# Convolution bias and gating bias taken off TensorE: added by VectorE, with the shifted weights made on ScalarE and GpSimd

## The reference

```python
def conformer_conv(a, gate, conv_w, conv_b, ln_g, ln_b):
    u = a * jax.nn.sigmoid(gate)
    u = lax.conv_general_dilated(            # depthwise, 31 taps, 512 channels
        u, conv_w[:, None, :], window_strides=(1,), padding=[(15, 15)],
        dimension_numbers=('NWC', 'WIO', 'NWC'), feature_group_count=D_A) + conv_b
    return jax.nn.silu(layernorm(u, ln_g, ln_b))

def spatial_gating(u, v, v_ln_g, v_ln_b, spatial_w, spatial_b):
    # out = u * (W_s norm(v) + b) within chunks of 128 positions, 4 heads of 128
    vn = layernorm(v.reshape(bn, s, N_SGU, H_D), v_ln_g, v_ln_b)
    vn = vn.reshape(bn, s // CHUNK, CHUNK, N_SGU, H_D)
    sv = jnp.einsum('hqk,bnkhc->bnqhc', spatial_w, vn) + spatial_b.T[:, :, None]
    return u * sv.reshape(bn, s, D_D)
```

## Time and profile before

| | us |
|---|---|
| median of 3 runs | 2552.85 |
| profiled execution, its own time | 2555.56 |
| its span, first to last instruction, slowest core | 2553.8 |
| spans of the 8 cores | 2547.6 to 2553.8 |

### The profile page before, as it was taken

How to read it: one execution, slowest core, us unless ns; L and a number is a source line. 1 busy time by engine, 2 the same in 40 slices (tenths; PEclk the granted TensorE clock), 3 DMA queues, 4 the chain that set the end, 5 groups by cost and what they waited for, 6 DMA issues and landing times.

```text
span 2553.8 us, 38161 instructions; the slowest of 8 cores (2547.6 to 2553.8 us)
## 1 busy us (share of the span) xinstructions
PE 2516.9 (99%) x12591; PEld 1184.0 (46%) x12591; DVE 894.7 (35%) x1454; ACT 619.6 (24%) x1083; POOL 413.6 (16%) x708
## 2 busy tenths in 40 slices
PE   8999999999999999999999999999999999999998
PEld 5445444444444444444444474444444444444443
DVE  4487465222222222211234773232223222222112
ACT  4336341131211121111143453211111111111111
POOL 3212233011101110010124521110111011101100
PEclk9999999999999999999999999999999999999999
DMA  8976799766645994456362278983576457644522
GB/s 176 192 128 146 148 150 177 159 148 123 127 141 120 159 158 141 104 75 103 125 117 95 43 143 172 168 148 114 120 128 112 120 120 127 113 120 98 76 42 99
DMA packets 310221, 323.98 MB, mean 127 GB/s; under 512 B 146049, under 2 KB 268177, under 8 KB 309906
## 3 DMA queue, kind: packets, MB, share of 16 engines
q0 software_dynamic: 123488, 121.41, 34.0%
q1 hardware_dynamic: 181506, 195.40, 28.0%
q10 hardware_dynamic: 5040, 4.73, 0.6%
HBM read 325.96 MB, written 79.69 MB: 159 GB/s over the span
## 4 chain that ended last, share of the span: by engine, by line
PE 95%; DVE 2%; DMA 1%; issue 1%; ACT 1%; POOL 0%; DVEq 0%; ACTq 0%; POOLq 0%
PE ps L171 95%; DMA wd<-ffn_wd 1%; DMA w_in<-ev_w_in 0%; DVE bst L1005 0%; DVE psum_w L755 0%; ACT BIG L1025 0%; ACT vn L1025 0%; DVE hb L379 0%; DVE gT L496 0%; DVE vt L1359 0%; ACT tmp L494 0%; DVE mv L1008 0%; DVEq L33 0%; DVE bst L1344 0%; DVE A L410 0%
## 5 line engine op out<-in xcount | busy, mean ns | idle before, releaser
L171 PE MATMUL ps<-BIG,wgu 128*128 128x512 bf16 x5632 | 1226.2, 379 | 0.0
L171 PEld LDWEIGHTS ps<-BIG,wgu 128*128 128x128 bf16 x5632 | 550.6, 98 | 662.7 <-issue 1.1
L171 PE MATMUL ps<-wd,gT 128*128 128x512 bf16 x2816 | 610.9, 380 | 2.1 <-DMA wd<-ffn_wd 2.1
L496 DVE TENSOR_TENSOR gT<-tmp,ps 128x512 bf16<-128x512 f32 x352 | 242.0, 687 | 812.7 <-PE ps L171 780.4
L171 PEld LDWEIGHTS ps<-wd,gT 128*128 128x128 bf16 x2816 | 276.0, 98 | 335.7 <-issue 4.5
L494 ACT ACTIVATE tmp<-ps 128x512 f32<-128x512 f32 x352 | 209.1, 594 | 782.4 <-PE ps L171 719.7
L185 POOL DMA_DIRECT2D wgu<-ffn_wgu x176 | 134.1, 762 | 848.4 <-PE ps L171 820.0
L171 PE MATMUL ps<-w_out,BIG 128*128 128x512 bf16 x1024 | 233.3, 381 | 8.6 <-DVE gT L496 6.0
L171 PE MATMUL ps<-w_in,BIG 128*128 128x512 bf16 (+1 forms) x1104 | 231.5, 365 | 4.0 <-DVE xr L521 1.5
L373 ACT ACTIVATE hb<-xr 128x1024 bf16<-128x1024 f32 x80 | 84.5, 1057 | 553.4 <-DVE xr L521 278.6
L357 POOL TENSOR_TENSOR ssb<-ssb,epsd 128x1 f32<-128x1 f32 x159 | 34.3, 216 | 1010.9 <-ACT hb L373 633.0
(11 more groups left out here) (145 smaller groups left out, 1136.9 us busy)
## 6 DMA issues: line engine op xcount, KB each, us to landing
wgu<-ffn_wgu POOLq DMA_DIRECT2D x176, 512.0 KB, 6.4
xr<-xr SPq DMA_DIRECT2D x59, 512.0 KB, 4.1
xr<-xres SPq DMA_DIRECT2D x32, 512.0 KB, 4.7
xnat<-xr SPq DMA_DIRECT2D x32, 512.0 KB, 3.5
out<-xr SPq DMA_DIRECT2D x31, 512.0 KB, 2.9
xr<-x SPq DMA_DIRECT2D x30, 512.0 KB, 6.3
xres<-xr SPq DMA_DIRECT2D x30, 512.0 KB, 3.9
xr<-xnat SPq DMA_DIRECT2D x27, 512.0 KB, 6.9
```

The source lines that it names most:

```text
L171: ins = self.nc.tensor.matmul(o, lhsT=l, rhs=r, start=st, stop=sp)
L496: k.op(dve, lambda e: e.tensor_tensor(out=gT[:, j, tg * 512:(tg + 1) * 512], in0=tmp[:], in1=ps[:, bl[1], :], op=ALU.mult), reads=[d_tmp, ...
```

## The change

The two bias matmuls per tile are taken out. For the convolution, `brow` becomes a map with the bias row in all 128 partitions, and the copy out of PSUM moves from ScalarE to VectorE as an addition of that map. The weight sets are split over three engines: 0, 1 and 15 stay on VectorE; 2, 5, 8, 11 and 14 go to GpSimd in the same form; 3, 4, 6, 7, 9, 10, 12 and 13 go to ScalarE, each as eight activations of 128 x 192 with one column of the mask as scale. The mask is loaded a second time, in float32, on ScalarE's queue. For the gating, `od_setup` multiplies `blT` and `sbrow` once and keeps the result as a map `sbt` in SBUF; per tile VectorE adds the map to the four matmuls' result into one of two buffers `svr`, and GpSimd multiplies by `uT` into `BIG`.

```diff
-            if t == 12: k.dma(pool, [(brow[0:1, :], T["ev_conv_b"])], writes=[d_brow])
+            if t == 12: k.dma(pool, [(brow[:], T["ev_conv_b"])], writes=[d_brow])
+                k.dma(act, [(mask32[:], T["mask"])], writes=[d_mask32])
...
         def wgen(i):
-            w = Wc[i % 4]
-            k.op(dve, lambda e: e.tensor_tensor(
+            w = Wc[i % 4].rearrange("p g j c -> p (g j) c")
+            src = wsh[:, 4 * i:4 * i + 4, :].rearrange("p g j -> p (g j)")
+            if i in WACT:
+                for c in range(8):
+                    k.op(act, lambda e: e.activation(out=w[:, :, c], in_=src, func=AF.Copy, scale=mask32[:, c:c + 1]),
+                         reads=[d_wsh, d_mask32], **({"addw": [d_Wc[i % 4]]} if c else {"writes": [d_Wc[i % 4]]}))
+                return
+            k.op(pool if i in WPOOL else dve, lambda e: e.tensor_tensor(
...
+        WPOOL = (2, 5, 8, 11, 14)
+        WACT = (3, 4, 6, 7, 9, 10, 12, 13)
...
         def conv(i, blk):
-            mms = [(ps[:, b, :], onesr[0:1, :].to_broadcast([1, 128]), brow[0:1, 32 * i:32 * i + 32] ..., True, False)]
+            mms = []
...
-            evac(0, z[blk][:, :, 32 * i:32 * i + 32].rearrange("q o (g c) -> q g o c", c=8),
-                 ps[:, b, :].rearrange("q (g o c) -> q g o c", g=4, c=8), [psd[b]], addw=d_z[blk])
+            k.op(dve, lambda e: e.tensor_tensor(
+                out=z[blk][:, :, 32 * i:32 * i + 32].rearrange("q o (g c) -> q g o c", c=8),
+                in0=ps[:, b, :].rearrange("q (g o c) -> q g o c", g=4, c=8),
+                in1=brow[:, 32 * i:32 * i + 32].rearrange("q (g c) -> q g c", c=8).unsqueeze(2)
+                .to_broadcast([128, 4, 16, 8]), op=ALU.add), reads=[psd[b], d_brow], addw=d_z[blk])
...
+        svr = ring("svr", 202 * KB, [512], F32, 2)
...                                                     (end of od_setup)
+            b = k.banks(1)
+            k.mm([(ps[:, b, :], blT[0:8, :], sbrow[0:8, :], True, True)], reads=[d_sbrow, d_blT], writes=[psd[b]])
+            t_, d_ = k.buf("sbt", o + 4096, [512], F32)
+            evac(1, t_[:], ps[:, b, :], [psd[b]], [d_])
...                                                     (sv)
-            mms = [(ps[:, b, :], blT[0:8, :], sbrow[0:8, :], True, False)]
...
-            k.op(dve, lambda e: e.tensor_tensor(out=BIG[:, t, 4:8, :], in0=ps[:, b, :].rearrange("p (h q) -> p h q", h=4),
-                                                in1=uT[:, r, :, ti * 128:(ti + 1) * 128], op=ALU.mult),
+            g, d_g = svr.next()
+            tt(g, ps[:, b, :], sbt[0][0][:], ALU.add, [psd[b], sbt[0][1]], writes=[d_g])
+            k.op(pool, lambda e: e.tensor_tensor(out=BIG[:, t, 4:8, :], in0=g.rearrange("p (h q) -> p h q", h=4),
+                                                 in1=uT[:, r, :, ti * 128:(ti + 1) * 128], op=ALU.mult),
```

More of the change, by code:

```diff
@@ L266 @@
     "ev_conv": [6, 128, 512],
-    "ev_conv_b": [1, 512],
+    "ev_conv_b": [128, 512],
     "ev_vec": [128, 3, 4],
@@ L669, in build @@
         brow, d_brow = k.buf("brow", 205 * KB, [512], BF16)
-        onesr, d_onesr = k.buf("onesr", sm + 224, [1], BF16)
         maskf, d_mask = k.buf("mask", sm + 240, [8], BF16)
         pwT, d_pwT = k.buf("pwT", sm + 256, [4, 128], BF16)
+        mask32, d_mask32 = k.buf("mask32", sm0 + 496, [8], F32)
         hx, d_hx = k.buf("hx", sm0 + 432, [4, 8], BF16)
@@ L676, in build @@
         U, d_U = k.lazy("U", 64 * KB, [64, 16, 8], BF16, 2)
-        k.op(dve, lambda e: e.memset(onesr[:], 1.0), writes=[d_onesr])
         def late_consts(t):
@@ L683, in late_consts @@
                 k.dma(pool, [(maskf[:], T["mask"])], writes=[d_mask])
-                k.dma(pool, [(brow[0:1, :], T["ev_conv_b"])], writes=[d_brow])
+                k.dma(pool, [(brow[:], T["ev_conv_b"])], writes=[d_brow])
                 k.dma(pool, [(pwT[:], T["ev_pool_wT"])], writes=[d_pwT])
                 k.dma(act, [(evec[:], T["ev_vec"])], writes=[d_evec])
+                k.dma(act, [(mask32[:], T["mask"])], writes=[d_mask32])
                 for v in (0, 272):
@@ L968, in wgen @@
         def wgen(i):
-            w = Wc[i % 4]
-            k.op(dve, lambda e: e.tensor_tensor(
-                out=w.rearrange("p g j c -> p (g j) c"),
-                in0=wsh[:, 4 * i:4 * i + 4, :].rearrange("p g j -> p (g j)").unsqueeze(2).to_broadcast([128, 192, 8]),
+            w = Wc[i % 4].rearrange("p g j c -> p (g j) c")
[6 more added lines that the diff above has]
+            k.op(pool if i in WPOOL else dve, lambda e: e.tensor_tensor(
+                out=w, in0=src.unsqueeze(2).to_broadcast([128, 192, 8]),
                 in1=maskf[:].unsqueeze(1).to_broadcast([128, 192, 8]), op=ALU.mult),
                 reads=[d_wsh, d_mask], writes=[d_Wc[i % 4]])
+        WPOOL = (2, 5, 8, 11, 14)
+        WACT = (3, 4, 6, 7, 9, 10, 12, 13)
         wgen(0)
@@ L982, in conv @@
             b = k.banks(1)
-            mms = [(ps[:, b, :], onesr[0:1, :].to_broadcast([1, 128]),
-                    brow[0:1, 32 * i:32 * i + 32].rearrange("o (g c) -> o g c", c=8).unsqueeze(2)
-                    .to_broadcast([1, 4, 16, 8]), True, False)]
+            mms = []
             for gl in range(4):
@@ L989, in conv @@
                     mms.append((ps[:, b, gl * 128:(gl + 1) * 128], UT[:, i // 2, 4 * (i % 2) + gl, c0:c0 + 128],
-                                Wc[i % 4][:, gl, dq * 16:(dq + 1) * 16, :], False,
-                                gl == 3 and dq == 2))
-            k.mm(mms, reads=[d_brow, d_onesr, d_Wc[i % 4], d_UT[i // 2][0], d_UT[i // 2][1]], writes=[psd[b]])
-            evac(0, z[blk][:, :, 32 * i:32 * i + 32].rearrange("q o (g c) -> q g o c", c=8),
-                 ps[:, b, :].rearrange("q (g o c) -> q g o c", g=4, c=8), [psd[b]], addw=d_z[blk])
+                                Wc[i % 4][:, gl, dq * 16:(dq + 1) * 16, :], dq == 0, dq == 2))
+            k.mm(mms, reads=[d_Wc[i % 4], d_UT[i // 2][0], d_UT[i // 2][1]], writes=[psd[b]])
+            k.op(dve, lambda e: e.tensor_tensor(
[3 more added lines that the diff above has]
+                .to_broadcast([128, 4, 16, 8]), op=ALU.add), reads=[psd[b], d_brow], addw=d_z[blk])
         bst, d_bst = k.buf("bst", sm, [4, 6], F32, 1)
@@ L1305, in build @@
         sc = 1.0 / np.sqrt(4096.0 * 128.0)
+        sbt = []
+        svr = ring("svr", 202 * KB, [512], F32, 2)
         def od_setup():
@@ L1322, in od_setup @@
                  reads=[d_sb8], writes=[d_sbrow])
+            b = k.banks(1)
+            k.mm([(ps[:, b, :], blT[0:8, :], sbrow[0:8, :], True, True)], reads=[d_sbrow, d_blT], writes=[psd[b]])
+            t_, d_ = k.buf("sbt", o + 4096, [512], F32)
+            sbt.append((t_, d_))
+            evac(1, t_[:], ps[:, b, :], [psd[b]], [d_])
         def u_quarter(tg, c):
@@ L1370, in sv @@
             b = k.banks(1)
-            mms = [(ps[:, b, :], blT[0:8, :], sbrow[0:8, :], True, False)]
[L1372 to L1375, removed]
-            k.op(dve, lambda e: e.tensor_tensor(out=BIG[:, t, 4:8, :], in0=ps[:, b, :].rearrange("p (h q) -> p h q", h=4),
-                                                in1=uT[:, r, :, ti * 128:(ti + 1) * 128], op=ALU.mult),
-                 reads=[psd[b]] + d_uT4[r], writes=[dB[t][1]])
+            k.mm([(ps[:, b, h * 128:(h + 1) * 128], vn[:, t % 6, h * 128:(h + 1) * 128], swT[:, h, :], True, True)
+                  for h in range(4)], reads=[d_vn[t % 6], d_swT], writes=[psd[b]])
+            g, d_g = svr.next()
+            tt(g, ps[:, b, :], sbt[0][0][:], ALU.add, [psd[b], sbt[0][1]], writes=[d_g])
+            k.op(pool, lambda e: e.tensor_tensor(out=BIG[:, t, 4:8, :], in0=g.rearrange("p (h q) -> p h q", h=4),
+                                                 in1=uT[:, r, :, ti * 128:(ti + 1) * 128], op=ALU.mult),
+                 reads=[d_g] + d_uT4[r], writes=[dB[t][1]])
         nev = [0]
@@ L1577, in prep_inputs @@
     g["ev_conv"] = runs(pad[16 * (dq - 1) + p - o + 15 + 32, 8 * gg + c].reshape(128, 64 * 48))
-    g["ev_conv_b"] = f(inputs["ev_conv_b"])[0].reshape(1, 512)
+    g["ev_conv_b"] = _rep(f(inputs["ev_conv_b"])[0])
     vecs = np.stack([f(inputs["ev_ln_g"])[0], f(inputs["ev_ln_b"])[0], f(inputs["ev_pool_scale"])[0].reshape(512)])
```

## The result

The changed kernel is slower by 1.1%: the ratio to the kernel before is 1.011, 95% interval 1.0094 to 1.0127, about 28 us. The profiled execution took 2580.88 us (span 2579.4) against 2555.56 before (span 2553.8), 25.3 us more.

What follows compares the result with a forecast made beforehand. TensorE, busy 99% of the span, was taken as the bound. Convolution -0.2 and gating -0.3 gave -0.5 us against the median of 2552.85: 2552 us; forecast's own range 2548 to 2556, with rivals 2543 to 2562.

Steps and rivals of the forecast that it cites:

- the price of ScalarE's activation: Convolution weight sets: 0.34 us per 128x192 activation, between 0.23 and 0.47; a set of eight 2.75 us.
- sets of ScalarE ... over 3.8: Convolution stage: sign that would prove the forecast wrong, a ScalarE weight set taking over 3.8 us (2.75 forecast).
- slower rival: Gating stage: GpSimd's product takes longer than 1.27 us, waiting for the ports; 2558 at 1.7, 2567 at 2.15; chance 0.22.
- The block without bias: Convolution stage: without its bias matmul of 0.32 us a TensorE block falls from 1.09 to 0.78 us.
- steps 5 to 15: Gating loop: TensorE steps of 5.5 us and above, GpSimd keeps up, so 11 x 0.315 = 3.5 us is kept.
- Set 2 behind w_out: Convolution start: GpSimd makes set 2 only after issuing w_out's loading, ready at 198.3; TensorE waits 4.9 us, its clock then falls.
- GpSimd's set: Convolution stage: one weight set of 128x1536 on GpSimd takes 3.5 us with the semaphore.
- VectorE's eviction: Convolution stage: each of 32 copies out of PSUM with the bias takes VectorE 0.68 us.
- The tail: End of convolution: last evictions, LayerNorm statistics, root, normalisations and SiLU; blocks end 223.6, TensorE goes on at 231.6 without clock fall.
- The gating stage: Second half of the change: 10.1 us of bias matmuls removed, nearly all lost to new waits; sum -0.3 us.
- Map: Gating set-up: one matmul of 0.31 us plus a TensorE wait of 1.75 us for sbrow; together +2.1 us.
- steps 16 to 27: Gating loop: GpSimd's 4.35 us step sets the pace, 54.2 against TensorE's 47.5; TensorE waits 4.8 us, 3.8 saved.

Runs made afterwards that it cites:

- a_const: The changed kernel with the scale of ScalarE's weight-set activations a constant 1.0 instead of a mask column in SBUF; time 2584.18 us.
- c_assign: c_major with sets 2 and 3 made on VectorE ahead of the loop, the others redistributed over ScalarE and GpSimd; ratio 0.9972 to the kernel before.
- c_major: The changed kernel with weight sets laid out channel first, so that no engine writes them with a step; ratio 0.9997 to the kernel before.
- v_steps: The changed kernel with sets 3 to 14 as eight 128x192 one-operand products on VectorE, GpSimd and ScalarE, with and without 16-byte steps; no time given.

## Why the prediction was wrong

- **The failed step is the price of ScalarE's activation.** The forecast put 128x192 between 0.23 and 0.47 us and took 0.34. It was 0.86. Without the step it is 0.35: the size was right for an instruction that the kernel did not issue, and that by some luck: 0.34 was the middle between the bounds, taken because one of two operands stands in SBUF, and with a constant in that operand's place (a_const) the spacing stayed at 0.85. All rows that served as bounds write elements that lie side by side in runs; `out=w[:, :, c]` writes single bf16 elements 16 bytes apart, and the bounds from both sides left that out. Put into the forecast's own working: eight sets of 6.85 from 191.5, with two evictions of 0.4 between, end at 247.1, and TensorE went on at 248.0. Seven blocks, begun at a clock of 0.50, took 7.24 instead of 5.5: the end of the stage at 255.1.
- The forecast named the sign itself ("sets of ScalarE ... over 3.8" as what would prove it wrong), but gave it no rival; its slower rival was GpSimd's product, which took 1.16 and not 1.27.
- **The block without bias** is shorter than forecast: 48 matmuls in 2.84 us make 0.67 a block, not 0.78. The bias matmul held 0.42 us, not 0.32, the difference of 1.09 and 0.67. In the convolution stage it gave nothing, because TensorE then waits; in gating steps 5 to 15 it gave its whole 0.42 a step.
- **Set 2 behind w_out**: wait 4.64 (4.9 forecast). The trace of the core shown names ScalarE as the one waited for, that of core 1 GpSimd (below); on the core shown GpSimd's set 2 ended 0.6 ahead of TensorE (191.91 + 2.80), and with set 2 on VectorE the wait is gone (c_assign), so it was that set. The clock fell to 0.57, as forecast.

```profile
194.90 1.98 PE L171 MATMUL ps<-Wc,UT 128*128 128x128 bf16 x24 [4.34 <-POOL Wc L976]
```

- **GpSimd's set** was 2.75, not 3.5; **VectorE's eviction** 0.685 (0.68). **The tail** in c_major is as forecast: 8.3 us from the end of the blocks (224.3) to 232.6, against 8.0.
- **The gating stage** gained 3.4 and not 0.3. Map: 1.90 (1.75). Steps 5 to 15 (first sv to the twelfth) took 71.5 us instead of 76.2, a gain of 4.7 (3.5). The main difference is in steps 16 to 27: 49.0 instead of 51.0, a gain of 2.0, where a loss of 1.0 was forecast. GpSimd's step there is 4.04 (1432.71, 1436.73, 1440.76 ...), not 4.35, because the product is 1.16 and the next instruction follows at once; over 12 steps that is 3.7. That GpSimd has hardly a gap there, that TensorE waits for vn in some of the steps (1.03 at 1437.13, 0.36 behind the end of a vn), and that the normalisation is held up (worst 1777 ns, mean 427 against 355), was right.

GpSimd's timeline after, one step of the gating loop:

```profile
1440.76 1.16 POOL L1391 TENSOR_TENSOR BIG<-svr,uT 128x512 bf16<-128x512 f32 x1
1441.88 0.20 POOL L357 TENSOR_TENSOR rs<-mv,cst 128x4 f32<-128x4 f32 x1
1442.22 1.19 POOL L359 TENSOR_TENSOR rs<-rs,cst 128x4 f32<-128x4 f32 x1
1443.58 1.27 POOL L1380 TENSOR_TENSOR vn<-vt,vln 128x512 bf16<-128x512 f32 x1 [0.17 <-DVE vt L1375]
1444.81 1.16 POOL L1391 TENSOR_TENSOR BIG<-svr,uT 128x512 bf16<-128x512 f32 x1
```

## What to carry to other kernels

When an instruction is priced by its neighbours, compare how its operands lie in memory, not only the size and the type: one step of 16 bytes in a bf16 output cost two and a half times the price, and the kernel 26 us. It was not all that kept the change from a gain: without the step the ratio was 0.9997, and only with the first sets out of the queue behind the w_out transfer 0.9972. Before a wide broadcast product that writes side by side is split into narrow ones that step, price the step; if it must be split, turn the layout so that the step falls on a side that has time (here TensorE's read and the eviction, at no cost that showed). And a short stall of TensorE is to be priced with the clock that may fall behind it.

## What the runs showed of the hardware

ScalarE's bf16 write of 192 elements: 0.35 us at 2 and 4 bytes from element to element, 0.43 at 8, 0.85 at 16. The two dear ones fit a price for each separate piece of 16 bytes: 192 pieces in 0.85 us are 4.4 ns a piece, and at 8 bytes 96 pieces by 4.4 are 0.43. At 4 bytes 48 pieces would be 0.21, under the 0.35 that the instruction takes in any case. That is a reading of four points, not shown beyond them. The Trainium skill tells of such a mechanism in "SBUF — State Buffer", section "Door 1: The DMA port swizzle": SBUF has lines of 16 bytes, and an access that goes on to a new line each time pays a penalty. The runs agree in that one element in each line is dear. They differ in two points: the page counts a step of 8 bf16, which is these 16 bytes, as free, and it asks for two hits in a line for full speed, but at 8 bytes, two in each line, the write still took 0.43 instead of 0.35.

VectorE and GpSimd kept each other waiting in several places where both worked from SBUF to SBUF. The scaling of the gamma row, 0.68 us elsewhere, took 2.73 in c_major while GpSimd made a set (207.72 to 210.47):

```profile
208.29 2.73 DVE L337 TENSOR_SCALAR gbc<-gbc 128x1024 f32<-128x1024 f32 x1
```

In v_steps both engines had rows of eight short products side by side. VectorE's stepped row (193.75 to 199.69) kept GpSimd out until its end: GpSimd's first product, started at 195.71, took 4.87, and 4.86 to 4.90 on the eight cores. The other way round it was mixed. Beside GpSimd's stepped products VectorE's eight without a step mostly got in by twos, and the row took 4.12 us; in one place the first two, 0.25 us alone, stood together for 8.36 and 8.23, as long as GpSimd's whole row, and VectorE's row took 9.48. That happened once in the sixteen places of this kind (two sets on eight cores).

```profile
L984 POOL TENSOR_SCALAR Wc<-wsh,mask x32: 760/1456/4874, 195.7 to 238.1; 128x192 bf16<-128x192 bf16 x32
...
202.06 4.12 DVE L984 TENSOR_SCALAR Wc<-wsh,mask 128x192 bf16<-128x192 bf16 x8
...
217.96 9.48 DVE L984 TENSOR_SCALAR Wc<-wsh,mask 128x192 bf16<-128x192 bf16 x8
```

The Trainium skill, "SBUF — State Buffer", section "SBUF: two separate sides", has the holder keep the ports for one instruction. The pairs that got in agree with it; the rows of eight that kept the other engine out for longer are what these runs add, and why it is at times one and at times the other is open.
